# A streaming encoder layer on eight cores: pooling emitted under the v projections, contiguous loads, transposes ahead, table copies dealt out, last tiles in halves

## The reference, cut to what matters

```python
h = rms_norm(x, norm_g)                                   # x: (B, T, 1024)
u, g_pool, v_a, v_b, g_conv = split(h @ w_in, 5 x 512)
pooled = (mean of the last 2/4/8/16 frames of u, by channel group of 128) - u
pool_out = silu(g_pool) * (pooled @ pool_mix[group]) * pool_scale
v = v_a * sigmoid(v_b)
c = causal depthwise convolution of v over 31 frames + dw_b
c = silu(layer_norm(c)) @ pw_w + pw_b
y = x + concat(pool_out, silu(g_conv) * c) @ w_out
out = rms_norm(y, final_g)
```

## Time and profile before

| | us |
|---|---|
| median of 3 runs | 307.74 (307.1 to 309.55) |
| the profiled execution, its own time | 309.66 |
| its span, slowest core (core 0) | 308.6 |
| spans of the eight cores | 300.3 to 308.6 |
| PE busy | 264.2 (86%) |
| DVE busy | 182.7 (59%) |
| ACT busy | 148.8 (48%) |
| POOL busy | 42.5 (14%) |
| moved by DMA | 44.38 MB |

### The profile page before, as it was taken

One profiled execution on the slowest core, in us unless ns is written; L12 is line 12 of the kernel. 1 busy time (PEld: TensorE's weight loads), 2 busy tenths in 40 slices (PEclk: granted clock), 3 DMA queues, 4 the chain that ended last, 5 costly groups with the idle time before them and its releaser, 6 DMA issues.

```text
span 308.6 us, 4619 instructions; the slowest of 8 cores (300.3 to 308.6 us)
## 1 busy us (share of the span) xinstructions
PE 264.2 (86%) x1768; PEld 144.2 (47%) x1768; DVE 182.7 (59%) x323; ACT 148.8 (48%) x271; POOL 42.5 (14%) x68
## 2 busy tenths in 40 slices
PE   4456988798696999999699379999999999999970
PEld 1356645644452544444356245454544454454430
DVE  1442043355437899999985047544665677567663
ACT  3233353566674329963157382583553343452221
POOL 0107223212310000004100000210020020110110
PEclk9998999999997999999979859999999999999997
DMA  7999995400499861355499301910333634546563
GB/s 157 297 325 310 306 309 171 130 2 2 72 133 147 148 120 25 98 121 121 88 147 166 82 0 19 280 42 2 99 115 131 218 122 143 199 153 204 203 208 136
DMA packets 22041, 44.38 MB, mean 144 GB/s; under 512 B 9633, under 2 KB 13345, under 8 KB 21634
## 3 DMA queue, kind: packets, MB, share of 16 engines
q1 hardware_dynamic: 21154, 39.16, 43.3%
q0 software_dynamic: 720, 4.85, 10.5%
q10 hardware_dynamic: 144, 0.07, 0.1%
HBM read 38.00 MB, written 10.93 MB: 159 GB/s over the span
## 4 chain that ended last, share of the span: by engine, by line
PE 56%; DVE 19%; ACT 11%; issue 6%; DMA 5%; POOL 2%; ACTq 0%; DVEq 0%; POOLq 0%; SPq 0%
PE PS L372 51%; PE PS L376 5%; DVE PA L357 4%; DMA WTAB<-wtab 4%; ACT HT L354 3%; DVE PL L368 3%; DVE HG L368 3%; DVE PB L357 2%; ACT WT L354 2%; POOL STAT L357 2%; ACT HG L424 2%; ACT JUNKB L424 2%; DVE VST L368 2%; DVE XR L357 1%; DMA ID<-ident 1%
## 5 line engine op out<-in xcount | busy, mean ns | idle before, releaser
L372 PE MATMUL PS<-HT,WIN 128*128 128x512 bf16 (+1 forms) x832 | 154.5, 346 | 15.9 <-ACT HT L354 9.3
L372 PEld LDWEIGHTS PS<-HT,WIN 128*128 128x128 bf16 x832 | 74.7, 104 | 83.5 <-ACT HT L354 10.6
L424 ACT ACTIVATE JUNKB<-XR 128x1024 bf16<-128x1024 f32 x16 | 16.9, 1057 | 52.6 <-DVE XR L357 52.6
L354 ACT ACTIVATE WT<-WTAB,PP 128x384 bf16<-128x384 f32 x64 | 33.6, 605 | 12.2 <-DMA WTAB<-wtab 12.2
L357 POOL TENSOR_TENSOR STAT<-STAT,NEGH 128x1 f32<-128x1 f32 (+2 forms) x34 | 18.5, 545 | 148.4 <-DVE STAT L361 148.4
L372 PE MATMUL PS<-WOUT,PL 128*128 128x512 bf16 x128 | 32.9, 379 | 0.0
L372 PE MATMUL PS<-WOUT,MIXC 128*128 128x512 bf16 x128 | 32.8, 379 | 0.0
L361 DVE TENSOR_SCALAR STAT<-STAT 128x1 f32<-128x1 f32 (+2 forms) x34 | 5.2, 152 | 43.8 <-ACT HG L424 22.7
L368 DVE SCALAR_TENSOR_TENSOR HG<-XA,STAT,GB 128x1024 bf16<-128x1024 f32 x16 | 22.2, 1389 | 11.2 <-POOL STAT L357 11.2
L354 ACT ACTIVATE HT<-PS 128x1024 bf16<-128x1024 bf16 x16 | 16.5, 1030 | 24.8 <-PE PS L376 24.8
L357 DVE TENSOR_TENSOR XR<-PS,XR 128x512 f32<-128x512 f32 x32 | 22.0, 688 | 8.5 <-PE PS L372 8.5
(11 more groups left out here) (101 smaller groups left out, 268.6 us busy)
## 6 DMA issues: line engine op xcount, KB each, us to landing
XA<-xp SPq DMA_DIRECT2D x16, 512.0 KB, 17.9
XR<-xp SPq DMA_DIRECT2D x16, 512.0 KB, 3.5
yp<-XR SPq DMA_DIRECT2D x16, 512.0 KB, 2.7
STG<-w_in SPq DMA_DIRECT2D x12, 512.0 KB, 16.8
vdram<-VST SPq DMA_DIRECT2D x4, 520.0 KB, 6.4
VS<-vdram SPq DMA_DIRECT2D x4, 520.0 KB, 7.0
WIN<-w_in POOLq DMA_DIRECT2D x2, 1024.0 KB, 17.7
WOUT<-w_out POOLq DMA_DIRECT2D x1, 2048.0 KB, 24.1
```

The costliest lines, as they stand in the source:

```text
L354: S.op('act', lambda e: e.activation(out=out, in_=in_, func=func, **kw), reads=reads, writes=writes)
L372: S.op('pe', lambda e: e.matmul(out, lhsT=lhsT, rhs=rhs, start=start, stop=stop), reads=reads, writes=writes)
L424: S.op('act', lambda e: e.activation(out=junk, in_=xt, func=AF.Square, scale=1.0 / 32.0, accum_out=ss[0:npart, :]), reads=[xk, 'STAT'], wr ...
```

## The change

- The arrays x, `w_in`, the tables and the output are laid out by tile or block, so that each load or store of 512 KB (192 KB) is one contiguous piece of DRAM.
- Of the loads, x1 comes second, x2 and x3 earlier, w blocks 3 and 7 ahead of x4 and x5.
- The epsilon of `rms` is added on POOL instead of DVE.
- The transposes of a tile are emitted a tile ahead of the u matmuls that use it; `v_unit` can take something between its two projections. x8's are made in quarter 1.
- The units of tile 'h' are merged: four column blocks in one bank, with one evacuation (`u_h`, `v_h`, `gp_h`, `gc_h`).
- v(1,2) and v(1,3) move behind the first u of quarter 3. Pooling items are emitted from there on under the v units, `conv_sample` is spread, and the rest is emitted before the second half of the gate units of group 2.
- Four table buffers. Tables 0 to 2 are loaded ahead, 3 and 4 under v(2,·), 5, 7 and 6 behind the last shuffle. Copies are emitted by five for each conv chunk, in a row over chunks 4 to 7.
- Six XR buffers. Tiles 12 to 15: each half of 512 columns has its own addition, square and gain product (DVE, into new buffers XF); POOL adds the two sums; ACT scales the halves (DVE the last); the last two tiles are stored in halves, one of them from ACT's queue.

```diff
-    xp_d = din("xp", (2048, 1024))
+    xp_d = din("xp", (NPH, 128, 1024))
-    win_d = din("w_in", (128, 20, 8, 128))
+    win_d = din("w_in", (20, 128, 1024))
-    wt_d = din("wtab", (128, NCHUNK, 384))
+    wt_d = din("wtab", (NCHUNK, 128, 384))
-    yp_d = dout("yp", (2048, 1024))
+    yp_d = dout("yp", (NPH, 128, 1024))
...
-            ts(ss[0:npart, :], ss[0:npart, :], EPS_RMS, ALU.add, [ssk], [ssk])
+            ts(ss[0:npart, :], ss[0:npart, :], EPS_RMS, ALU.add, [ssk], [ssk], eng='pool')
...
+        def proj_h(m0, n):
+            b, bk = psum()
+            for c in range(4):
                 for k in range(8):
-                    mm(PSB_[b][:, 0:n], wk(m, k), HTH[:, k, 0:n], k == 0, k == 7, [wkey[m], 'HTH'], [bk])
-            else:
-                hk = ['HT%d' % (4 * q + j) for j in range(4)]
-                for k in range(8):
-                    mm(PSB_[b][:], wk(m, k), HT[:, q, k, :], k == 0, k == 7, [wkey[m]] + hk, [bk])
-            return PSB_[b], bk
+                    mm(PSB_[b][:, c * n:(c + 1) * n], wk(m0 + c, k), HTH[:, k, 0:n], k == 0, k == 7,
+                       [wkey[m0 + c], 'HTH'], [bk])
+            return PSB_[b][:, 0:4 * n].rearrange("p (c t) -> p c t", c=4), bk
+
+        def u_h():
+            acc, bk = proj_h(MU, 64)
+            act(US[:, :, :, 16:32], acc[:, :, 0:32].rearrange("p c (s t) -> p c s t", s=2), AF.Copy, [bk],
+                ['USn%d' % c for c in range(4)])
+            act(U[:, :, :, 0:1].rearrange("p c a b -> p c (a b)"), acc[:, :, 33:64:2], AF.Copy,
+                [bk], ['U%dh' % c for c in range(4)])
+
+        def v_h():
+            acc, bk = proj_h(MVB, 64)
+            th = ['THH%d' % c for c in range(4)]
+            act(THH[:], acc, AF.Tanh, [bk], th, scale=0.5)
+            acc2, bk2 = proj_h(MVA, 64)
...
+        wslot = (0, 1, 2, 0, 1, 2, 3, 0)
+
         def load_wt(ch):
-            load(WTAB[ch % 2][:].rearrange("p a b -> p (a b)"), wt_d[:, ch, :], 'WTAB%d' % (ch % 2),
-                 'wtab%d' % (ch % 2))
+            i = wslot[ch]
+            load(WTAB[i][:].rearrange("p a b -> p (a b)"), wt_d[ch], 'WTAB%d' % i, 'wtab%d' % i)
 
         def build_wt(ch, js=range(8)):
-            s = ch % 4
+            s, i = ch % 4, wslot[ch]
             for j in js:
-                act(WT[s][:, :, j * 16:(j + 1) * 16], WTAB[ch % 2][:], AF.Copy, ['PP', 'WTAB%d' % (ch % 2)],
+                act(WT[s][:, :, j * 16:(j + 1) * 16], WTAB[i][:], AF.Copy, ['PP', 'WTAB%d' % i],
                     ['WT%d_%d' % (s, j)], scale=PP[:, 13 + j:14 + j])
-            if 7 in js and ch + 2 < NCHUNK:
-                load_wt(ch + 2)
...
+            for i, p in enumerate(range(NPH - 4, NPH)):
+                q, pq = p // 4, p % 4
+                xr, xk, sc = XR[p % 6], 'XR%d' % (p % 6), 56 + 4 * i
+                for hf in range(2):
+                    sl = slice(hf * 512, hf * 512 + 512)
+                    b, bk = psum()
+                    for e_ in range(8):
+                        if e_ < 4:
+                            lh, lk = PL[:, e_, p, :], 'MIXP%d_%d' % (q, e_)
+                        else:
+                            lh, lk = MIXC[q % 2][:, e_ - 4, pq * 128:(pq + 1) * 128], 'MIXC%d_%d' % (q % 2, e_ - 4)
+                        mm(PSB_[b][:], lh, WOUT[:, e_, sl], e_ == 0, e_ == 7, [lk, 'WOUT'], [bk])
+                    pk, fk, ssk = '%s_%d' % (xk, hf), 'XF%d_%d' % (i, hf), 'SSL%d' % (sc + hf)
+                    tt(xr[:, sl], PSB_[b][:], xr[:, sl], ALU.add, [bk, xk], [pk])
+                    S.op('act', lambda e, sl=sl, c=sc + hf, xr=xr: e.activation(
+                        out=JUNKB[:, sl], in_=xr[:, sl], func=AF.Square, scale=1.0 / 32.0,
+                        accum_out=STAT[:, c:c + 1]), reads=[pk, 'STAT'], writes=[ssk, 'JUNKB'])
+                    if pend_scale:
+                        pend_scale.pop(0)()
+                    if i == 0 and hf == 1:
+                        fin_pend()
+                    tt(XF[i][:, sl], xr[:, sl], FGB[:, sl], ALU.mult, [pk, 'FGB'], [fk])
+                    if hf == 0:
+                        ts(STAT[:, sc:sc + 1], STAT[:, sc:sc + 1], EPS_RMS, ALU.add, [ssk], [ssk], eng='pool')
+                tt(STAT[:, sc:sc + 1], STAT[:, sc:sc + 1], STAT[:, sc + 1:sc + 2], ALU.add,
+                   ['SSL%d' % sc, 'SSL%d' % (sc + 1)], ['SSL%d' % sc], eng='pool')
+                rs, rsk = STAT[:, sc + 2:sc + 3], 'RSL%d' % i
+                tt(rs, STAT[:, sc:sc + 1], NEGH[:, 0:1], ALU.pow, ['SSL%d' % sc, 'NEGH', 'STAT'], [rsk], eng='pool')
+
+                def scale(hf, i=i, p=p, rs=rs, rsk=rsk):
+                    sl = slice(hf * 512, hf * 512 + 512)
+                    fk = 'XF%d_%d' % (i, hf)
+                    if p == NPH - 1 and hf == 1:
+                        ts(XF[i][:, sl], XF[i][:, sl], rs, ALU.mult, [fk, rsk], [fk])
+                    else:
+                        act(XF[i][:, sl], XF[i][:, sl], AF.Copy, [fk, rsk], [fk], scale=rs)
+                    if p >= NPH - 2:
+                        S.op('act' if p == NPH - 1 and hf == 0 else 'sp',
+                             lambda e: e.dma_start(out=yp_d[p][:, sl], in_=XF[i][:, sl]),
+                             reads=[fk], writes=['o_yp%d_%d' % (p, hf)], dma='stl%d%d' % (p % 2, hf))
+                    elif hf == 1:
+                        S.op('sp', lambda e: e.dma_start(out=yp_d[p], in_=XF[i][:]), reads=['XF%d_0' % i, 'XF%d_1' % i],
+                             writes=['o_yp%d' % p], dma='st%d' % (p % 6))
+                pend_scale += [lambda f=scale: f(0), lambda f=scale: f(1)]
+            while pend_scale:
+                pend_scale.pop(0)()
...
         load(ID32[:], id_d, 'ID32', 'c_id', 'act')
+        load_x(1)
         stage_win(8, 'sp')
         stage_win(9, 'sp')
-        load_x(1)
+        load_x(2)
         stage_win(10, 'sp')
+        load_x(3)
         stage_win(11, 'sp')
-        load_x(2)
-        load_x(3)
-        for m in (0, 4, 1, 5, 2, 6):
+        for m in (0, 4, 1, 5, 2, 6, 3, 7):
             stage_win(m, 'sp')
         load_x(4)
         load_x(5)
-        stage_win(3, 'sp')
-        stage_win(7, 'sp')
...
@@ -826,20 +898,25 @@
         utile, uout = u_tiles(0)
         pre(0)
         cast_win(8, 'dve')
+        pre(1)
+        trans(0)
         cast_win(9, 'dve')
-        trans(0)
-        pre(1)
-        utile(0, (0, 1))
         cast_win(10, 'dve')
+        utile(0, (0,))
+        trans(1)
+        utile(0, (1,))
+        utile(1, (0, 1))
+        pre(2)
+        utile(0, (2,))
+        utile(1, (2,))
         cast_win(11, 'dve')
-        trans(1)
-        pre(2)
-        utile(0, (2, 3))
+        pre(3)
         trans(2)
-        pre(3)
-        utile(1)
+        utile(0, (3,))
+        utile(1, (3,))
+        utile(2, (0, 1))
         trans(3)
-        utile(2)
+        utile(2, (2, 3))
         utile(3)
...
-        for m in (0, 4, 1, 5, 2, 6):
+        for m in (0, 4, 1, 5, 2, 6, 3, 7):
             cast_win(m, 'pool')
         v_unit(0, 0)
         v_unit(0, 1)
         pre(4)
         v_unit(0, 2)
         pre(5)
-        cast_win(3, 'pool')
-        cast_win(7, 'pool')
+        v_unit(0, 3, lambda: trans(4))
+        pre(6)
         utile, uout = u_tiles(1)
-        trans(4)
+        trans(5)
+        pre(7)
         utile(0)
-        trans(5)
+        for p in range(12, 14):
+            load_x(p)
+        trans(6)
         utile(1)
-        pre(6)
-        v_unit(0, 3)
-        pre(7)
-        trans(6)
+        pre(8)
+        trans(7)
         utile(2)
-        trans(7)
+        pre(9)
+        for p in range(14, 16):
+            load_x(p)
+        cache_in()
+        trans(8)
         utile(3)
+        pre('h')
         uout()
-        cache_in()
-        for p in range(12, 16):
-            load_x(p)
-        pre(8)
+        pre(10)
         v_unit(1, 0)
-        pre(9)
+        trans(9)
+        pre(11)
+        pre(12)
         v_unit(1, 1)
-        pre('h')
-        trans(8)
-        pre(10)
-        v_unit(1, 2)
-        trans(9)
         trans('h')
-        pre(11)
-        v_unit('h', 0)
-        v_unit('h', 1)
-        v_unit(1, 3)
-        v_unit('h', 2)
-        v_unit('h', 3)
+        trans(10)
+        trans(11)
+        v_h()
+        pre(13)
+        pre(14)
         v_halo(0)
         v_shuffle(0)
-        v_halo(1)
-        v_shuffle(1)
+        u_unit(2, 0)
+        trans(12)
+        u_unit(2, 1)
+        pre(15)
         S.op('pool', lambda e: e.dma_start(out=PMW[:], in_=pmw_d), writes=['PMW'], dma='wpm')
         load_win(12, 16, 'wgp')
         load_win(16, 20, 'wgc')
-        trans(10)
-        pre(12)
-        trans(11)
-        pre(13)
-        u_unit(2, 0)
-        u_unit(2, 1)
-        trans(12)
-        pre(14)
+        trans(13)
         u_unit(2, 2)
-        trans(13)
-        pre(15)
-        u_unit(2, 3)
-        for c in range(4):
-            u_unit('h', c)
         load_wt(0)
         load_wt(1)
+        load_wt(2)
         trans(14)
+        u_unit(2, 3)
```

(72 more changed lines are left out.)

122 lines of the change are left out of this document (65 added, 57 removed).

## The result

The changed kernel takes 278.29 us, the median of 4 runs (278.22 to 278.43), where the kernel before took 307.83 on the same chip (307.1 to 309.55, 4 runs): a ratio of 0.903, with a 95% interval of 0.8985 to 0.9076. The forecast was 278.0.

What follows compares the result with a forecast made beforehand. PE was taken as the bound in the dense last stretch, DVE from 99.86 to 157.85. Gains 8.6 + 6.5 + 3.6 + 10.2 + 3.0 = 31.9 off 309.66 gave 277.8, forecast 278 us; own range 274 to 282, 8 in 10 within 271 to 291.

Steps and rivals of the forecast that it cites:

- Start and first two quarters: Head through quarter 1's u: new load order and earlier transposes end it at 53.2 instead of 61.8, gaining 8.6 us.
- Contiguous blocks (0): DRAM layout of the loads: contiguous blocks gain nothing; bounds were no change or 3 us at the end.
- Third quarter and halo: From there to u of quarter 3: 20.7 us, with ACT ending last, instead of 27.2; gain 6.5.
- Pooling under v: Up to the conv chunks: pooling on DVE runs under the v units; 6.1 less 2.5 gives a gain of 3.6 us.
- The lag of 1.5 on DVE: At conv chunk 2: PE waits 1.5 us for DVE's pooling, taken off the gain.
- the 1.0 of the shuffle: Before chunk 0: writing and reading back VS of quarter 3 has no cover left; 1.0 us taken off the gain.
- Tables: Conv chunks: early loads into four buffers remove the 6.63 us stall and 3.6 of half rate behind it; gain 10.2.
- the bound of five copies: Conv chunks: ACT keeps up with PE's 3.28 us a chunk with five copies (3.1), not with eight (4.7).
- Tail: Behind the last matmul: finishing the last tiles in halves takes 6.3 us instead of 9.3; gain 3.0.
- Rival 5: Last tiles: POOL steps and DVE's gain products exclude each other, so the tail gains 1.8, total 279; chance 0.1.
- Rivals 1, 2 and 4: Costs feared: ACT or loads lag, 287 (0.18); late shuffle and first tables, 284 (0.08); lower clock, 319 at 0.85 (0.04).
- Rival 3: Loads: contiguous blocks load faster, giving 274.5 us in total; chance 0.07.

Runs made afterwards that it cites:

- the last kernel: Changed kernel with VS32's scaling moved just ahead of v_h and three table copies ahead of chunk 0's gate unit: 274.0 us against 276.3, slowest of cores 0 to 3.

## Why the prediction was right

The total was right, at 278.0 against 278.29, and so were the mechanisms of the steps, with two exceptions: the blocks that the forecast expected to land alike, and the engine that ends the third quarter. The sizes were off by up to 2.7 us in both directions, and that they cancel is luck. Between the same points of the two slowest cores' traces:

| part | forecast | measured |
|---|---|---|
| start and first two quarters | 8.6 | 9.8 |
| third quarter and halo (to u of quarter 3) | 6.5 | 4.4 |
| pooling under v (to chunk 1) | 3.6 | 6.3 |
| tables (to the first gc unit) | 10.2 | 7.9 |
| from the first gc unit to the last matmul | 0 | −0.3 |
| tail | 3.0 | 3.3 |
| sum | 31.9 | 31.4 |

The 6.9 of v(1,2) and v(1,3) is counted where each kernel has them. The 31.4 is the difference of the two spans, 308.6 and 277.2.

- **Start and first two quarters, 8.6.** Measured 9.8 (61.8 against 52.04). With the old layout x4 and the end of quarter 1's u are where the forecast put them, so the step was right for the landings that it assumed. What it lacked is the step **Contiguous blocks (0)**, which failed: undone, the layout costs 3.1. The bound of "3 us at the end" was in the text, and I took its other end because x's and w_in's blocks landed alike; both were then in one queue, where w_in's blocks stood ahead of x4. The Trainium skill (DMA: Bandwidth & Descriptors, Latency and other measured facts) reports a loss from row steps of 512 KiB up and has no row for smaller ones; here steps of 80 KB in w_in brought x4's square 2.9 us later, and steps of 64 KB in x did not move it. Its bandwidth per core in the HBM Reference (Specifications (TRN2)), 358 GB/s, is not contradicted: slices of the page reach 342.
- **Third quarter and halo, 6.5.** The stage took 23.3 where I had 21.1. "ACT is what ends last here" was true for 0.8 of it, PE's wait for the copies of U, and wrong by an engine for the rest: POOL's queue held the halo's power behind the scaling of the cache. I had moved `cache_in` in the order and followed its DMAs, not its POOL instruction. On the other seven cores the stage took 21.8 to 22.4; core 3 is the one that met the POOL wait in full, 1.5, and it was the slowest.
- **Pooling under v, 3.6.** Chunk 0 at 134.01 against 133.8. The lag of 1.5 on DVE and the 1.0 of the shuffle, both taken off the gain, did not come: PE waits for no PL and no VS, and 6.3 were gained where 6.1 was the sum without them. (The 4.4 in that step's heading does not follow from its terms; the sum used 3.6.) For the lag the step took 63.4 us, the length of the stretch, as DVE's work, where the rows have DVE busy for 60.1 of it; DVE's last pooling operation then ended at 138.55 and not at 140.3. Undone, the part costs 9.0, since it also covers the gates' weights and the first table.
- **Tables, 10.2.** In the stage 7.9; undone 7.2, alone about 5. The mechanism was right (the stall is gone) and the size was off. The matmuls behind the stall lost 2.9 and not 3.6: in the trace of before the next gate unit starts at 185.23, 6.16 behind the end of the wait, where 3.28 is usual. A new 1.59 is to be taken off as well, and the bound of five copies had no ground. For the 5 alone the reason is in the next paragraph.
- **Tail, 3.0.** 3.3, with 6.0 behind the last matmul where I had 6.3. POOL's add took 0.19 and the power 0.57. Rival 5 did not happen there, as the two never met: DVE's last gain product had ended at 272.63, before POOL's add at 272.81.
- **Rivals 1, 2 and 4.** No wait of PE for ACT over 1.2 in the middle stages, no wait for VS or for a table on PE's side until the last chunk, and a granted clock of 1.00 in every stretch: none of the three came to cost time. One sign that I had named failed even so: ACT did wait for a table, the first, 2.9 on core 3 and 2.6 to 4.8 on five of the cores, without a wait of PE. Rival 3, faster loads, did happen, with about the price that I gave it, hidden in the total by the 1.5 of POOL and the 1.6 of the weights.

**The terms don't add.** Undone one at a time, the parts cost 3.1 + 3.3 + 7.2 + 9.0 + 20.2 = 42.8 us, for a gain of 29.5. The layout and the tables, the two that were also tried alone, are worth more once the others are there. I also read the old kernel on its slowest core, and a stall of 6.63 there is 2.3 on another; without it another core ends last.

What stays open: why x's layout costs 0.5 to 1.0 without moving x4; how the 9.0 of the late pooling divides between DVE and the loads; and how the copies by eight and the moved scaling do together.

## What to carry to other kernels

Before a term is taken from the slowest core's trace, read the same wait on the other cores: a stall behind a loaded DMA queue has a different size on each, and the gain is that of the core that is slowest afterwards. When an operation is moved past others, list all engines on which it issues: one POOL instruction of 1.2 us that waited for a load cost up to 1.5 on the slowest core and nothing on others, because a power that PE needed was queued behind it. A unit that stands between two others may be the cover of a copy or a load, so price its removal as well as its arrival.

## What the runs showed of the hardware

- **One queue, two layouts.** With the 512 KB blocks of w_in as 128 rows of 4 KB at a step of 80 KB, x4, behind them in the queue, was squared at 36.0 to 36.9 where it was 33.2 to 34.5 with contiguous ones, and the span of cores 0 to 3 was 2.6 to 3.1 longer. With x at a step of 64 KB x4's square stayed at 32.9 to 34.8, and the span was 0.5 to 1.0 longer. What makes the two unlike was not tried.
- **POOL beside DVE.** A power on one column takes 0.57, and 1.43 when it meets a DVE product with two SBUF inputs, as on core 3 of the changed kernel:

```profile
58.25 1.43 POOL L363 TENSOR_TENSOR STAT<-STAT,NEGH 128x1 f32<-128x1 f32 x1
```

```profile
57.96 1.28 DVE L374 SCALAR_TENSOR_TENSOR HG<-XH,STAT,GB 64x1024 bf16<-64x1024 f32 x1 [6.01 <-POOL STAT L363]
```

  The power starts within the product and ends 0.44 behind its end, and the product keeps its 1.28. An epsilon on one column went from 0.22 to 1.32 in the last kernel, beside such a product. By the Trainium skill (SBUF — State Buffer, SBUF: two separate sides) such a pair excludes each other, which agrees. The forecast looked for this in the tail, and it was in the middle.
